# Reordering both ends of an encoder layer and moving additions from VectorE to GpSimd

## What is computed

```python
h = rmsnorm(x, mix_norm_g)
q, k, v, f = split(h @ w_in)              # 2048 -> 3*2048 + 16 heads
q, k = rmsnorm(q, g_q), rmsnorm(k, g_k)    # per head of 128
c = cumsum(log_sigmoid(f + b_f))
s = q @ k.T * 128**-0.5 + c_query - c_key  # causal
x = x + softmax(s) @ v @ w_out
h = rmsnorm(x, ffn_norm_g)
gate, up = split(h @ w_gate_up)            # 2048 -> 2 * 5632
x = x + (silu(gate) * up) @ w_down         # 5632 -> 2048
```

## Time and profile before

| | |
|---|---|
| time, median of 3 runs | 2122.63 us (2122.53 to 2127.16) |
| the profiled execution | 2121.12 us |
| its span, first to last instruction | 2119.2 us |
| TensorE, products | 2107.2 us busy (99%) |
| VectorE | 1524.0 us busy (72%) |
| ScalarE | 943.2 us busy (45%) |
| GpSimd | 193.1 us busy (9%) |
| mean granted clock of TensorE | 0.998 |

### The profile page before, as it was taken

One profiled execution on the slowest core, in us unless ns is written; L12 is line 12 of the kernel. 1 busy time (PEld: TensorE's weight loads), 2 busy tenths in 40 slices (PEclk: granted clock), 3 DMA queues, 4 the chain that ended last, 5 costly groups with the idle time before them and its releaser, 6 DMA issues.

```text
span 2119.2 us, 28267 instructions
## 1 busy us (share of the span) xinstructions
PE 2107.2 (99%) x10400; PEld 1846.6 (87%) x10400; DVE 1524.0 (72%) x2106; ACT 943.2 (45%) x1279; POOL 193.1 (9%) x355
## 2 busy tenths in 40 slices
PE   9999999999999999999999999999999999999998
PEld 8999999999998888888888888888888888888887
DVE  4565566565555435988888888887988977969978
ACT  6333333333344335454444444454444564554533
POOL 0332332233221000000000000000000000000000
PEclk9999999999999999999999999999999999999999
DMA  6465655665234334665766666666667877868866
GB/s 187 118 191 185 211 184 189 201 195 181 79 115 148 113 118 142 204 214 186 236 208 202 222 220 197 218 213 212 205 224 230 287 269 244 269 219 268 268 192 210
DMA packets 269053, 422.45 MB, mean 199 GB/s; under 512 B 17011, under 2 KB 116373, under 8 KB 265637
## 3 DMA queue, kind: packets, MB, share of 16 engines
q1 hardware_dynamic: 248048, 354.24, 53.1%
q10 hardware_dynamic: 20916, 67.01, 8.8%
HBM read 369.52 MB, written 51.68 MB: 199 GB/s over the span
## 4 chain that ended last, share of the span: by engine, by line
PE 98%; DMA 1%; DVE 1%; issue 0%; ACTq 0%; SPq 0%; DVEq 0%
PE gemm L592 11%; PE gemm L594 11%; PE gemm L593 11%; PE gemm L798 11%; PE gemm L796 11%; PE gemm L797 11%; PE aux L796 8%; PE aux L798 8%; PE aux L797 8%; PE aux L593 1%; PE aux L594 1%; PE aux L592 1%; PE aux L847 1%; PE aux L646 1%; PE aux L618 0%; DMA f_raw<-in_ffn_w_gate_up 0%
## 5 line engine op out<-in xcount | busy, mean ns | idle before, releaser
L1476 DVE TENSOR_TENSOR f_lo<-f_raw,f_hi 128x1536 fp32r<-128x1536 f32 (+1 forms) x230 | 454.5, 1980 | 73.1 <-ACT f_hi L1130 40.4
L592 PE MATMUL gemm<-w_hi,act_t 128*128 128x384 f32 (+2 forms) x1280 | 450.9, 352 | 0.5 <-issue 0.5
L593 PE MATMUL gemm<-w_lo,act_t 128*128 128x384 f32 (+2 forms) x1280 | 443.9, 347 | 0.0
L594 PE MATMUL gemm<-w_hi,act_t 128*128 128x384 f32 (+2 forms) x1280 | 443.9, 347 | 0.0
L798 PE MATMUL gemm<-f_hi,a_form 128*128 128x512 f32 x1056 | 411.0, 389 | 0.0
L796 PE MATMUL gemm<-f_hi,a_form 128*128 128x512 f32 x1056 | 411.0, 389 | 0.0
L797 PE MATMUL gemm<-f_lo,a_form 128*128 128x512 f32 x1056 | 410.8, 389 | 0.0
L796 PE MATMUL aux<-f_hi,a_form 128*128 128x512 f32 x792 | 311.0, 393 | 0.7 <-DVE f_lo L1476 0.7
L798 PE MATMUL aux<-f_hi,a_form 128*128 128x512 f32 x792 | 308.4, 389 | 0.0
L797 PE MATMUL aux<-f_lo,a_form 128*128 128x512 f32 x792 | 308.2, 389 | 0.0
L1086 ACT ACTIVATE f_hi<-f_raw 128x1536 fp32r<-128x1536 f32 x132 | 196.2, 1486 | 217.4 <-DMA f_raw<-in_ffn_w_gate_up 88.0
(11 more groups left out here) (188 smaller groups left out, 2252.2 us busy)
## 6 DMA issues: line engine op xcount, KB each, us to landing
f_raw<-in_ffn_w_gate_up SPq DMA_DIRECT2D x264, 512.0 KB, 4.2
w_raw<-in_fox_w_in SPq DMA_DIRECT2D x189, 256.0 KB, 3.5
f_raw<-in_ffn_w_down SPq DMA_DIRECT2D x88, 512.0 KB, 4.7
f_raw<-in_ffn_w_gate_up SPq DMA_DIRECT2D x88, 256.0 KB, 4.0
f_raw<-t_scratch SPq DMA_DIRECT2D x44, 512.0 KB, 4.8
w_raw<-in_fox_w_out SPq DMA_DIRECT2D x16, 1024.0 KB, 5.1
pre_w<-in_ffn_w_down ACTq DMA_DIRECT2D x22, 512.0 KB, 5.2
pre_rows<-in_ffn_w_down ACTq DMA_DIRECT2D x22, 512.0 KB, 7.0
```

The lines of the kernel that those rows point to most:

```text
L592: mm(out, a_hi, b_hi, start=first, stop=False)
L593: mm(out, a_hi, b_lo, start=False, stop=False)
L594: return mm(out, a_lo, b_hi, start=False, stop=last)
L1476: v.tensor_tensor(f_lo[:, n % 4, 0:3 + g], f_raw[:, n % 4, 0:3 + g], f32(f_hi[:, n % 3, 0:3 + g]), ALU.subtract).then_inc(f_lo_done, 1)
```

## The change

- ScalarE's queue loads the mix gains before anything else, with a semaphore of their own. TensorE transposes them alone, then two quarters of x, then all the gains again into another bank; ScalarE copies the mix gains, the first piece of `act_t`, the other gains, and then splits the first weights before the second piece. The first chunk goes k by k over the four row blocks instead of in pairs of k, and VectorE interleaves likewise.
- The last two units run product by product (`last_two_units`): P6 and P5 of both, P7 of both, P4 of both, the last by row block. The low parts of the last unit are made in two halves.
- In the last round, GpSimd adds `p3_kept` into X3 and subtracts `junk_act` (P1) from X4, which VectorE did; VectorE's `add_p1` moves to j = 5, behind the low parts of the last unit. GpSimd also adds X4 to the kept x1 piece (`x1_u`) and X4 into X3 at the end; VectorE ends the two C22 blocks in `p2_kept`.
- The final stores go in another order.

```diff
             sp.dma_start(y_cols[0][:, 0:2], rows[:, 0, 0:2]).then_inc(y_stored, 16)
-            sp.wait_ge(x1_p1, NR - R_DOWN)
-            sp.dma_start(y_cols[1][:, 0:2], rows[:, 1, 0:2]).then_inc(y_stored, 16)
             sp.wait_ge(c_out, 2)
             sp.dma_start(y_cols[2][:, 0:2], rows[:, 2, 0:2]).then_inc(y_stored, 16)
             sp.wait_ge(x2_x4, 2)
             sp.dma_start(y_cols[0][:, 2:4], rows[:, 0, 2:4]).then_inc(y_stored, 16)
             sp.wait_ge(piece_added, 7)
             sp.dma_start(y_cols[2][:, 2:4], rows[:, 2, 2:4]).then_inc(y_stored, 16)
-            for t in range(2):
-                sp.wait_ge(c12_out, t + 1)
-                sp.dma_start(y_cols[3][:, t], rows[:, 3, t]).then_inc(y_stored, 16)
-            for t in range(2):
-                sp.wait_ge(c21_out, t + 1)
-                sp.dma_start(y_cols[1][:, 2 + t], rows[:, 1, 2 + t]).then_inc(y_stored, 16)
+            sp.wait_ge(x1_p1, NR - R_DOWN)
+            sp.dma_start(y_cols[1][:, 0:2], rows[:, 1, 0:2]).then_inc(y_stored, 16)
+            sp.wait_ge(c21_out, 1)
+            sp.dma_start(y_cols[1][:, 2], rows[:, 1, 2]).then_inc(y_stored, 16)
+            sp.wait_ge(c12_out, 1)
+            sp.dma_start(y_cols[3][:, 0], rows[:, 3, 0]).then_inc(y_stored, 16)
+            sp.wait_ge(c21_out, 2)
+            sp.dma_start(y_cols[1][:, 3], rows[:, 1, 3]).then_inc(y_stored, 16)
             sp.wait_ge(y_stored, 16 * (5 + 6))
...
+            pool.wait_ge(p3_read, 2 * NR)
+            pool.wait_ge(x3_p3, NR - R_DOWN - 3)
+            g.tensor_tensor(rows[:, 3, 0:2], rows[:, 3, 0:2], p3_kept[:], ALU.add).then_inc(x3_p3, 1)
+            pool.wait_ge(p5_read, 2 * (NR - 1))
+            pool.wait_ge(p1_read, 2 * NR)
+            g.tensor_tensor(rows[:, 3, 2:4], rows[:, 3, 2:4], junk_act[:], ALU.subtract).then_inc(x4_p1, 1)
+            pool.wait_ge(last_piece_ld, 16)
             for t in range(2):
-                pool.wait_ge(x3_p3, NR - R_DOWN - 2)
                 pool.wait_ge(x4_p5, t + 1)
+                g.tensor_tensor(p2_kept[:, t], p2_kept[:, t], rows[:, 3, 2 + t], ALU.add).then_inc(x1_u, 1)
+            pool.wait_ge(x3_p3, NR - R_DOWN - 2)
+            for t in range(2):
                 g.tensor_tensor(rows[:, 3, t], rows[:, 3, t], rows[:, 3, 2 + t], ALU.add).then_inc(c12_out, 1)
-            pool.wait_ge(x1_p7, 1)
-            g.tensor_tensor(rows[:, 3, 2], rows[:, 3, 2], p2_kept[:, 0], ALU.add).then_inc(c22_out[0], 1)
...
                 for half in range(2):
-                    for t in range(NT):
-                        if t == 0:
-                            pe.wait_ge(w_lo_done, half + 1)
-                            pe.wait_ge(tr_lo, 2 * half + 2)
-                        rows_slot(G[t], 0, 0, t, True, False, width, ks=(2 * half, 2 * half + 1))
-                        if half == 0 and t == 0:
+                    for k in (2 * half, 2 * half + 1):
+                        pe.wait_ge(w_lo_done, half + 1)
+                        pe.wait_ge(tr_lo, k + 1)
+                        for t in range(NT):
+                            rows_slot(G[t], 0, 0, t, True, False, width, ks=(k,))
+                        if k == 0:
                             pe.wait_ge(x_ld[0], 16)
...
             keep_warm(5)
-            pe.wait_ge(gain_ld, 16 * 4)
-            nc.tensor.transpose(G[0][:, 0:2 * NK + 2], gain_rows[:], ident[0:2 * NK + 2, 0:2 * NK + 2])\
-                .then_inc(gain_T, 1)
+            pe.wait_ge(mix_ld, 16)
+            nc.tensor.transpose(G[0][:, 0:NK], gain_rows[0:NK, :], ident[0:NK, 0:NK]).then_inc(gain_T, 1)
             pe.wait_ge(x_half_ld, 16)
             transpose_rows(0, 0, (0, 1))
+            pe.wait_ge(gain_ld, 16 * 3)
+            nc.tensor.transpose(G[2][:, 0:2 * NK + 2], gain_rows[:], ident[0:2 * NK + 2, 0:2 * NK + 2])\
+                .then_inc(gain_T, 1)
             keep_warm(6)
-            pe.wait_ge(gain_done, 1)
+            pe.wait_ge(gain_done, 2)
             first_chunk()
...
-            def product(n, form, weights, banks, wait_free, last):
+            def product(n, form, weights, banks, wait_free, last, tiles=range(2)):
                 r, g, j = UNITS[n]
                 hi, lo = f_hi[:, n % 3, weights], f_lo[:, n % 4, weights]
-                for t in range(2):
+                for t in tiles:
                     if j == 0:
...
-            for n in range(NU):
+            def last_two_units(n):
+                pe.wait_ge(f_lo_done, n + 1)
+                product(n, S2, 3, bank_a, free_p6, False)
+                product(n, S1, 0, bank_d, free_p5, False)
+                pe.wait_ge(f_lo_done, n + 2)
+                product(n + 1, S2, 3, bank_a, free_p6, False)
+                product(n + 1, S1, 0, bank_d, free_p5, False)
+                product(n, S3, 1, bank_b, free_p7, False)
+                product(n + 1, S3, 1, bank_b, free_p7, False)
+                for t in range(2):
+                    product(n, A22, 2, bank_c, free_p4, True, (t,))
+                    product(n + 1, A22, 2, bank_c, free_p4, True, (t,))
+            for n in range(NU - 2):
                 r, g, j = UNITS[n]
...
                     product(n, A22, 2, bank_c, free_p4, True)
+            last_two_units(NU - 2)
...
+            act.dma_start(gain_rows[0:NK, :], mix_g.rearrange("o (k p) -> (o k) p", p=P)).then_inc(mix_ld, 16)
             load_wf(0)
-            for dst, src in ((gain_rows[0:NK, :], mix_g.rearrange("o (k p) -> (o k) p", p=P)),
-                             (gain_rows[NK:2 * NK, :], ffn_g.rearrange("o (k p) -> (o k) p", p=P)),
+            for dst, src in ((gain_rows[NK:2 * NK, :], ffn_g.rearrange("o (k p) -> (o k) p", p=P)),
                              (gain_rows[2 * NK:2 * NK + 1, :], g_q),
...
             act.wait_ge(gain_T, 1)
-            a.activation(gain[:], G[0][:, 0:2 * NK + 2], ACT.Copy).then_inc(gain_done, 1)
+            a.activation(gain[:, 0:NK], G[0][:, 0:NK], ACT.Copy).then_inc(gain_done, 1)
             act.wait_ge(gain_done, 1)
+            transposed_hi(0, 0, 0)
+            act.wait_ge(gain_T, 2)
+            a.activation(gain[:, NK:2 * NK + 2], G[2][:, NK:2 * NK + 2], ACT.Copy).then_inc(gain_done, 1)
+            act.wait_ge(wf_ld[0], 16)
+            split_hi(0, 0, 0, in_proj=True, first=True)
+            transposed_hi(0, 0, 1)
+            act.wait_ge(gain_done, 2)
             a.activation(gain_q[:], gain[:, 2 * NK:2 * NK + 1], ACT.Copy, scale=float(HD) ** -0.5)
-            for half in range(2):
-                transposed_hi(0, 0, 2 * half)
-                transposed_hi(0, 0, 2 * half + 1)
-                if half == 0:
-                    act.wait_ge(wf_ld[0], 16)
-                split_hi(0, 0, half, in_proj=True, first=True)
-                if half == 0:
-                    for kg in range(1, KG):
-                        load_wf(kg)
+            for kg in range(1, KG):
+                load_wf(kg)
+            split_hi(0, 0, 1, in_proj=True, first=True)
+            transposed_hi(0, 0, 2)
+            transposed_hi(0, 0, 3)
             for kg in range(KG):
...
                 act.wait_ge(c22_out[t], 1)
-                act.dma_start(y_cols[3][:, 2 + t], rows[:, 3, 2 + t]).then_inc(y_stored, 16)
+                act.dma_start(y_cols[3][:, 2 + t], p2_kept[:, t]).then_inc(y_stored, 16)
+            act.wait_ge(c12_out, 2)
+            act.dma_start(y_cols[3][:, 1], rows[:, 3, 1]).then_inc(y_stored, 16)
...
             v.tensor_copy(causal_r[:], causal[:]).then_inc(causal_done, 1)
-            for half in range(2):
-                transposed_lo(0, 0, 2 * half)
-                transposed_lo(0, 0, 2 * half + 1)
-                split_lo(0, 0, half, QKV, first=True)
+            transposed_lo(0, 0, 0)
+            split_lo(0, 0, 0, QKV, first=True)
+            transposed_lo(0, 0, 1)
+            split_lo(0, 0, 1, QKV, first=True)
+            transposed_lo(0, 0, 2)
+            transposed_lo(0, 0, 3)
             for kg in range(KG):
...
-            def take_last_p1(r):
-                x4 = rows[:, 3, 2:4]
-                dve.wait_ge(p5_read, 2 * r)
-                dve.wait_ge(p1_read, 2 * r + 2)
-                v.tensor_tensor(x4, x4, junk_act[:], ALU.subtract).then_inc(x4_p1, 1)
             def last_products(r):
-                dve.wait_ge(x3_p3, NR - R_DOWN - 2)
                 dve.wait_ge(x4_p1, NR - R_DOWN)
                 dve.wait_ge(x2_p5, 2 * (NR - 1 - R_DOWN))
-                dve.wait_ge(last_piece_ld, 16)
                 for t in range(2):
...
                 for t in range(2):
+                    x2 = rows[:, 1, 2 + t]
                     wait_product(dve, r, True, 4 + t)
-                    v.tensor_tensor(p2_kept[:, t], p2_kept[:, t], bank_b[t][:], ALU.subtract).then_inc(x1_p7, 1)
-                for t in range(2):
-                    x2 = rows[:, 1, 2 + t]
                     v.tensor_tensor(x2, bank_b[t][:], x2, ALU.add).then_inc(x2_p7, 1)
-                for t in range(2):
+                    dve.wait_ge(x1_u, t + 1)
```

(20 more changed lines are left out.)

## The result

The kernel before takes 2123.12 us (2122.11 to 2127.16), the changed one 2126.49 us (2124.28 to 2128.76): a ratio of 1.0015, 95% interval [1.0008, 1.0022]. That is 3.4 us more, within the 0.3% that the prediction called "same". The profiled execution of the changed kernel took 2128.76 us, with a span of 2127.0 us.

The account below looks back on a forecast made before the run. TensorE bounds the kernel. Head -0.6, tail -2.0 and hold-up +3.1 (relief of VectorE included) sum to +0.5: 2121.6 for the profiled execution, 2123.1 as median; own range 2122 to 2124.5, with rivals 2119.0 to 2126.5.

Parts of the forecast that it names:

- What bounds it: Whole kernel: TensorE busy 2107.2 of 2119.2 us; the body can only get longer, by starving TensorE; head and tail are open.
- One sign of being wrong: Body: the prediction is wrong if TensorE waits anywhere between 100 and 2077 us that it didn't before.
- Part 4, the hold-up: Last round: GpSimd's two additions each stop a VectorE operation 2.0 us; TensorE stalls 2.9 at unit 2; 3.1 us lost.
- data part of GpSimd's instruction: Last round: VectorE stands still for an addition's data time, 2.0 us for 1024 columns, not the whole 2.5.
- The 0.3 at unit 3: Last round: `f_lo` of unit 3 ready at 2093.1, so TensorE stalls 0.3 us more there.
- rival (b): After unit 2: the 2.9 us hole makes TensorE's clock fall, 1.7 us lost: 2124.4, or 2126 if twice; chance 0.25.
- Rival (a), no hold-up: Last round: GpSimd takes the holes and waits alone, VectorE isn't held up: -2.7 us, 2119.9; chance 0.25.
- Part 2, the tail: Last two units by product: span ends E + 5.25 against E + 7.2 (E: last product's end); 2.0 us gained, bounds 1.0 to 2.5.
- from there to the end it was 4.0 us, I keep 4.0: Tail: from VectorE's last addition to the span's end, last store and program end, stays 4.0 us.
- Part 1, the head: Before the first product: mix gains loaded and transposed first, product at 10.5 instead of 11.07; 0.6 us gained, bounds 0 to 1.0.
- the cover that I named: First chunk: `act_t` pieces 2 and 3 needed some 4 us after the first product, so later loads hide behind it.
- Part 3: Last round: VectorE relieved of additions; the 0.22 us stall goes, 0.1 comes at unit 6; 0.1 us gained.

Follow-up runs that it names:

- The head alone: The kernel before with only the change's hunks up to the first chunk of x, tail and last round as before: 2121.87 us, 0.9992.
- GpSimd's additions alone: The kernel before with only the two additions (P3 into X3, P1 from X4) moved to GpSimd, both ends as before: 2129.29 us, 1.0028.
- The one-input run: The changed kernel with GpSimd's two additions replaced by one-input operations of the same 1024 columns: 2122.83 us, 0.9998.
- second addition later: The changed kernel with GpSimd's second addition held back until unit 2 of the last half round is done: 2124.81 us, 1.0005.
- VectorE's reductions made the hole: The changed kernel with both additions on VectorE, plus two unused VectorE reductions of 2048 columns where GpSimd's additions had met it: 2126.74 us, 1.0016.
- The kernel with the stores spread: The changed kernel with both additions on VectorE, GpSimd's last four additions alternating between tasks and X3's first block stored earlier: 2121.65 us, 0.9994.
- the second trace of the changed kernel: The changed kernel, unaltered, measured and profiled once more: 2126.74 us, 1.0013 against the kernel before.
- with an addition less: The changed kernel with both additions on VectorE, P3 added into X3 only after the P5 additions: 2121.84 us, 0.9993.
- by writing alone: The changed kernel with GpSimd's two additions replaced by memsets of the same blocks: 2122.51 us, 0.9996.

## Why the prediction was right, and where it was off

**What bounds it**: right. Nothing could be won in the body, and the loss came from starving TensorE in the last round. One sign of being wrong did come: waits of TensorE between 100 and 2077 us that weren't there before (0.97 us at 1824, 0.64 at 1211). It was a bad sign to choose. The head alone, with its FFN as before, has such waits of up to 0.89 us, and GpSimd's additions alone have none over 0.3 in that stretch, so they don't come from the change in the last round.

**Part 4, the hold-up**: right in place, kind and size. Forecast were two sums of VectorE lengthened by 2.0 us each and a stall of 2.9 at unit 2; measured 2.20 and 2.08, and 3.0 to 3.2. The term "data part of GpSimd's instruction" was 5 to 10% small. The Trainium skill (SBUF — State Buffer, SBUF: two separate sides) has the whole instruction as the price: of GpSimd's 2.46 us VectorE lost 2.20, which lies between the two. The two-input traces can't tell them apart, since the sum started 0.12 us behind GpSimd's addition and went on as that ended, so it was held for nearly all that was left of it. The one-input run goes against the whole instruction: there a sum ran at its usual 0.69 us under GpSimd's. The 0.3 at unit 3 didn't come: the clock, low by then, had given VectorE the time back, as rival (b) had it. Where the clock stayed up (second addition later, one input), the products at unit 3 did lose 0.34 us. Rival (a), no hold-up, is refuted by every trace in which GpSimd adds beside those sums.

**Rival (b), the clock**: this is the step that failed. The forecast put the clock's loss behind the hole of 2.9 us at nothing, and the rows gave no reason for that: only holes of up to 0.5 us were in the trace of before. So I gave the fall 0.25 and the forecast without it 0.40. The runs showed 1.7 us and more in its place. It fell in all three traces that had both GpSimd additions where the change put them, once for 3.4 us in two of them (1.7 lost), for 6.8 in one (2.8 lost), and in the one where VectorE's reductions made the hole. Holes of 2.06, 3.03, 3.22, 3.25 and 3.36 us were followed by a fall; those of 1.78, 1.65, 1.11 us and less by none. With one fall rival (b) said 2124.4, with two 2126; the median is 2126.49. That this is near the case of two falls is luck: the trace with one fall took 2126.88 us, and the rest of the difference is in parts 2 and 3.

**Part 2, the tail**: the order worked, but the gain is 1.0 us (7.19 to 6.17), not 2.0. VectorE's last addition ends 1.16 behind TensorE, 1.3 forecast, and GpSimd ended at E + 0.9, forecast 1.0. The mis-sized term is "from there to the end it was 4.0 us, I keep 4.0": it was 5.0. Six stores of 256 KB leave within 3.3 us, three of them in the last 0.6, and the later ones take longer to land: 2.4, 2.7, 3.5, 3.2, 4.3 and 4.6 us. Before, six left within 3.3 us too, but the last three in 0.9, and the last took 3.5 us. The kernel with the stores spread bears this out in part: its last three leave in 0.6 us as well, but behind a longer gap (1.2 us, 0.8 in the changed kernel), its end is 5.55 us behind TensorE's, and 0.6 of the missing 1.0 us came back.

**Part 1, the head**: the first product came 1.2 us earlier (0.5 to 1.5 in all the traces with this head), forecast 0.6, bounds 0 to 1.0, so the gain was larger than the bound. But it is seldom kept: at the 193rd product 0.05 and 0.26 us is left in the traces of the changed kernel, and more than 0.5 us in two of the twelve traces with this head. What gives it back is the second chunk of x, whose weights and `act_t` come later; the cover that I named ("some 4 us, and they hide behind it") was read for the first chunk only. Why the third weight load lands at 16.7 in some executions and at 18.1 in others is open: the order of the `wf` loads is not the cause.

**Part 3**: forecast −0.1, measured +1.0. With the additions on VectorE the starts of the products at unit 6 lose 0.9 us (the wait of 0.65 and the start-up behind it), and the small stall at unit 5 stays (0.34, before 0.22); "last 200" shows it, 46.9 against 45.8. I had unit 6's `f_lo` ready 0.05 us after the need. Two limits lie on each other there: with the additions on VectorE that engine is never idle and ends `f_lo` at 2104.03, 0.75 us after the need, and with an addition less the load comes last, for the same wait.

**The sum** by what the traces show, for the second trace of the changed kernel: lead at the 193rd product −0.3, hole +3.4 (from start to start of the products), clock +1.7, units 5 and 6 +1.0, tail −1.0: +4.8. The medians differ by 3.4, and their interval, 0.0008 to 0.0022 of 2123, is 1.7 to 4.7 us. The sum is at its upper end; 1.4 us, less than the body's spread, has no term. Executions in which the clock doesn't fall may be a part of it. In the forecast +0.5 the two biggest errors were the clock (1.7 and more) and the two terms of 1.0 at the end, the stores and unit 6.

**Best version**: the changed kernel with both additions on VectorE, 2121.5 to 2121.7 us. It is 5 us below the changed kernel, and 1.5 below the kernel before, with intervals that reach over no difference.

## What to carry to other kernels

An engine that is 9% busy isn't free help: two GpSimd additions, of 2.46 and 3.38 us, put beside the engine that feeds TensorE, took 4.3 us from it, where on that engine they would have cost 2.4. Give GpSimd work that reads two SBUF tensors only where VectorE has slack of the same length, or where VectorE's operations take one operand from PSUM: in the tail those took their usual 0.68 us beside GpSimd's additions. If a hole can't be avoided, two short ones may be cheaper than one long one, since here the clock fell behind a hole of 3 us and not behind two of 1.8 and 1.0 (one trace).

## What the runs showed of the hardware

- GpSimd's reads stop a VectorE operation with two SBUF inputs, its writes don't: held for 2.20 and 2.08 us by 1024 columns with two inputs, 0.84 and 0.78 with one input, 0.00 by writing alone. With two inputs the hold lasted until GpSimd's instruction ended, with one input it ended earlier: the next sum ran its usual 0.69 us under the same instruction of 2.86 us.
- The stop works both ways: GpSimd's second addition took 3.38 us instead of 2.46, with the sum of VectorE ahead of it. And GpSimd gets in between two VectorE operations that follow each other with a gap of 0.04 us (2083.16 to 2083.20).
- Behind a hole TensorE's clock fell to 1.2 GHz at no fixed point: in one trace while TensorE was still idle (2089.11, the work went on at 2090.17), in the other four 0.2 to 1.2 us after the work had gone on. It stayed down for 3.4 us, in the first one for 6.8, with TensorE at full work.
- The body, the same work in all kernels, takes 2014.1 to 2019.7 us. Of this 1.7 us is a fall of the clock at 65 us, which 7 of the 14 traces have and 7 have not; some are waits at weight loads, at places that differ. Their cause is open.
